# Two feed-forward blocks, fused per hidden block, changed to an up phase and a down phase of Strassen block products

## The reference, cut to what matters

```python
# first block, its end
x = x + merged @ w_out
xn = rms_norm(x, ffn_norm_g)
gate, up = split(xn @ w_gate_up, 2)          # (1024, 1024) @ (1024, 2*2816)
x = x + (silu(gate) * up) @ w_down           # (1024, 2816) @ (2816, 1024)
x = rms_norm(x, final_norm_g)
# second block, its end
x = x + concat([y_sc, y_gdn, y_sb]) @ w_mix_out
h = rmsnorm(x, w_norm_ffn)
u = causal_dwconv(h @ w_ffn_up, w_ffn_conv)  # 3 taps per column
gate, val = split(u, 2)
x = x + (silu(gate) * val) @ w_ffn_down
x = rmsnorm(x, w_norm_final)
```

## Time and profile before

| | us |
|---|---|
| runs shown | 2682.76, 2685.54, 2688.26 |
| median | 2685.54 |
| span of the profiled execution | 2685.9 |
| first feed-forward loop, about 526 to 1206 us of the span | 680 |
| second feed-forward loop, about 1976 to 2660 us | 684 |

### The profile page before, as it was taken

One profiled execution on the slowest core, in us unless ns is written; L12 is line 12 of the kernel. 1 busy time (PEld: TensorE's weight loads), 2 busy tenths in 40 slices (PEclk: granted clock), 3 DMA queues, 4 the chain that ended last, 5 costly groups with the idle time before them and its releaser, 6 DMA issues. The chain is left out here.

```text
span 2685.9 us, 36806 instructions
## 1 busy us (share of the span) xinstructions
PE 2609.6 (97%) x13899; PEld 2081.9 (78%) x13899; DVE 1235.7 (46%) x1717; ACT 680.0 (25%) x1336; POOL 1181.7 (44%) x946
## 2 busy tenths in 40 slices
PE   8999889999999999999999988999999999999998
PEld 6787458888888888887788876845888888888877
DVE  3233543323333333345554155565235555555568
ACT  3200761200000000015233255465131111111123
POOL 4342144244444444463355541515425555555553
PEclk9999999999999999999999999999999999999999
DMA  4111103111111111122111200002101111111112
GB/s 136 44 48 43 48 15 112 32 47 47 50 48 50 47 47 47 51 75 94 32 51 47 59 2 2 18 1 102 51 24 49 49 47 51 47 47 51 47 55 79
DMA packets 92176, 133.83 MB, mean 50 GB/s; under 512 B 9397, under 2 KB 57760, under 8 KB 92072
## 3 DMA queue, kind: packets, MB, share of 16 engines
q1 hardware_dynamic: 89440, 123.86, 15.3%
q10 hardware_dynamic: 2632, 8.51, 0.8%
HBM read 123.92 MB, written 8.42 MB: 49 GB/s over the span
## 5 line engine op out<-in xcount | busy, mean ns | idle before, releaser
L115 POOL TENSOR_TENSOR w_hi<-w_raw,zero 128x512 fp32r<-128x512 f32 x328 | 388.3, 1184 | 989.0 <-PE bank L1100 450.5
L117 POOL TENSOR_TENSOR w_lo<-w_raw,w_hi 128x512 fp32r<-128x512 f32 x328 | 474.9, 1448 | 25.7
L1098 PE MATMUL bank<-xt_hi,w_hi 128*128 128x512 f32 x1232 | 479.5, 389 | 0.8 <-DVE x_sb L1331 0.8
L1100 PE MATMUL bank<-xt_hi,w_lo 128*128 128x512 f32 x1232 | 479.3, 389 | 0.0
L1099 PE MATMUL bank<-xt_lo,w_hi 128*128 128x512 f32 x1232 | 479.3, 389 | 0.0
L1435 DVE TENSOR_TENSOR x_sb<-bank,x_sb 128x512 f32<-128x512 f32 x320 | 221.2, 691 | 203.5 <-PE bank L1134 203.2
L1098 PEld LDWEIGHTS bank<-xt_hi,w_hi 128*128 128x128 f32 x1232 | 231.2, 188 | 49.2 <-DVE x_sb L1331 1.2
L1100 PEld LDWEIGHTS bank<-xt_hi,w_lo 128*128 128x128 f32 x1232 | 231.2, 188 | 48.1
L1099 PEld LDWEIGHTS bank<-xt_lo,w_hi 128*128 128x128 f32 x1232 | 231.2, 188 | 48.0
L1393 DVE COPY hidden_raw<-bank 128x512 f32<-128x512 f32 x44 | 30.4, 692 | 326.0 <-PE bank L1100 326.0
L1402 DVE SCALAR_TENSOR_TENSOR hidden_conv<-hidden_raw_conv,cols,hidden_conv 128x1024 f32<-128x1024 f32 x80 | 156.0, 1979 | 6.6 <-ACT hidden_conv L1235 1.3
(11 more groups left out here) (567 smaller groups left out, 4861.3 us busy)
## 6 DMA issues: line engine op xcount, KB each, us to landing
w_raw<-in_w_gate_up_dram SPq DMA_DIRECT2D x88, 256.0 KB, 3.1
w_raw<-in_w_ffn_up_dram SPq DMA_DIRECT2D x88, 256.0 KB, 3.1
w_raw<-in_w_mix_in_dram SPq DMA_DIRECT2D x64, 256.0 KB, 2.7
w_raw<-in_w_down_dram SPq DMA_DIRECT2D x44, 256.0 KB, 2.6
w_raw<-in_w_ffn_down_dram SPq DMA_DIRECT2D x44, 256.0 KB, 2.6
w_raw<-in_w_in_dram SPq DMA_DIRECT2D x40, 256.0 KB, 2.6
x_sb<-in_x_dram SPq DMA_DIRECT2D x4, 1024.0 KB, 8.4
gate_rows<-gate_sums SPq DMA_DIRECT2D x8, 512.0 KB, 5.5
```

The lines of the kernel that those rows point to most:

```text
L115: pool.tensor_tensor(m.w_hi[:, u, :], m.w_raw[:, u, :], zeros, ALU.add).then_inc(m.hi_done, 1)
L117: pool.tensor_tensor(m.w_lo[:, u, :], m.w_raw[:, u, :], m.w_hi[:, u, :].bitcast(F32), ALU.subtract).then_inc(m.split, 1)
L1098: pe.matmul(m.psum[b][:, :], u_hi[:, col], m.xt_hi[:, k, tok], start=k == 0, stop=False)
L1100: mm = pe.matmul(m.psum[b][:, :], u_lo[:, col], m.xt_hi[:, k, tok], start=False, stop=k == KD - 1)
```

## The change

Both calls of `mlp_stage` change in the same way. The loop over hidden blocks is replaced by two phases, each cut by Strassen's scheme: a product of 2x2 block matrices is made of seven block products (M1 to M7) of sums and differences of blocks instead of eight.

**Up phase.** 22 steps q (gate and up half of each hidden block), each in four units k, so 88 units. A unit takes one w_raw slice (rows k and k+4 of the weights, 256 columns), POOL makes five 128-column block sums of it (`sums`, three instructions, 640 elements), ACT rounds sums (640) and the two plain blocks (256) into `ring_hi`, POOL takes the rest into `ring_lo` (640 and 256). PE does 7 products of three matmuls with the sums of the transposed tokens, which are made once, in the head. ACT copies three products' banks and DVE adds the rest, eight adds for each q (`corners`). The gated rows of each hidden block go to DRAM (`hidden_between`), and the residual goes to DRAM in the head (`x_mid`). All loops are unrolled. With `conv`, middle tap, side taps and silu are as before (4 side taps of 128x1024 for each q).

**Down phase.** 7 products times 11 pairs of hidden blocks, 77 units, in two column groups c (7 pairs, then 4). A unit's operands are a token-side piece A (from `hidden_between`, stationary) and a weight-side piece B, 128x512 each, loaded from DRAM once for all products. POOL makes the sums that a product needs (`OP_A`, `OP_B`: 10 for each pair), ACT rounds both operands, DVE takes the rest of both (POOL of B for four of the products and even pairs: 24 of the 154), PE does 4 tiles of three matmuls. The banks of a finished product are added to one or two quarters of `acc` (`CORNERS`: 12 for each c, times 4 tiles). `acc` is loaded from `x_mid`.

**Head and end.** The head makes the token sums on DVE and POOL and their halves on ACT and DVE; the first q's products 2 and 4 are done on tokens 0 to 511 alone, then the other half is transposed, then products 5, 3, 1, 7, 6. The stage behind starts from other addresses. Semaphores are shared by both calls.

```diff
+PRODUCTS = (2, 4, 5, 3, 1, 7, 6)
...
+DOWN = (3, 5, 1, 4, 7, 2, 6)
...
+OP_A = {1: ("A11", "A22", ALU.add), 2: ("A21", "A22", ALU.add), 3: ("A11",), 4: ("A22",), 5: ("A11", "A12", ALU.add),
+        6: ("A21", "A11", ALU.subtract), 7: ("A12", "A22", ALU.subtract)}
+OP_B = {1: ("B11", "B22", ALU.add), 2: ("B11",), 3: ("B12", "B22", ALU.subtract), 4: ("B21", "B11", ALU.subtract),
+        5: ("B22",), 6: ("B11", "B12", ALU.add), 7: ("B21", "B22", ALU.add)}
+CORNERS = {1: ((0, 0, ALU.add), (1, 1, ALU.add)), 2: ((1, 0, ALU.add), (1, 1, ALU.subtract)),
+           3: ((1, 1, ALU.add), (0, 1, ALU.add)), 4: ((0, 0, ALU.add), (1, 0, ALU.add)),
+           5: ((0, 1, ALU.add), (0, 0, ALU.subtract)), 6: ((1, 1, ALU.add),), 7: ((0, 0, ALU.add),)}
...
+    def slot_free(eng, n):
+
+        if n >= 5:
+            ge(eng, wused, n - 4 if n <= 8 else n - 3)
+        elif n < 2 or n == (2 if lead is None else 4):
+            eng.wait_ge(m.used, base + 8)
+        else:
+            eng.wait_ge(m.used, base + 16)
+
...
+    def low_on_pool(x, p):
+
+        return x in (2, 3, 4, 5) and p % 2 == 0
...
+            def fetch(p, x):
+                place_, when = home[p, x]
+                if p < FIRST_PAIRS:
+                    ge(sp, wused, 5 if when < 0 else UP_UNITS - KQ + when + 1)
+                elif when is not None:
+                    n = at_unit[0, when[0], when[1]]
+                    ge(sp, lod, dve_lows(n))
+                    ge(sp, wlo, pool_lows(n))
+                if x[0] == "A":
+                    ge(sp, hid_out, 32 * (p + 1))
+                sp.dma_start(piece[p, x][:, :], piece_source(p, x)).then_inc(raw_in[p % FIRST_PAIRS].sem, 16)
...
+                fetch(p, "A12")
+            ge(sp, x_out, 16 * NT)
+            ge(sp, hid, 2 * FI)
+            fetch_acc(1, 1, 0)
...
-            split_slices(m, pool, loop, 12 * (FI - 2))
...
+            def sums(n):
+                if n >= UP_UNITS:
+                    gi, x, c, p = unit(n)
+                    to = stage[(n - UP_UNITS) % 3]
+                    if n < UP_UNITS + 3:
+                        ge(pool, wlo, 2 * (UP_UNITS - 1 if n == UP_UNITS else UP_UNITS))
+                    else:
+                        ge(pool, lod, dve_lows(n - 3))
+                        ge(pool, wlo, pool_lows(n - 3))
+                    pieces_in(pool, p, PIECES_OF[x])
+                    for side, op in ((0, OP_A[x]), (1, OP_B[x])):
+                        if len(op) == 3:
+                            pool.tensor_tensor(to[:, side, :], piece[p, op[0]][:, :], piece[p, op[1]][:, :],
+                                               op[2]).then_inc(summed.sem, 1)
+                    return
+                u, s = n % RING, n % 3
+                four = m.w_raw[:, u, :].rearrange("p (b n) -> p b n", b=4)
+                to = w_sum[:, s, :].rearrange("p (b n) -> p b n", b=5)
+                if n >= 3:
+                    ge(pool, wlo, 2 * (n - 2))
+                ge(pool, raw_in[u], 16 * (n // RING + 1))
+                pool.tensor_tensor(to[:, 0:2, :], four[:, 0:2, :], four[:, 3:4, :].to_broadcast([P, 2, P]),
+                                   ALU.add).then_inc(summed.sem, 1)
+                pool.tensor_tensor(to[:, 2:4, :], four[:, 1:3, :], four[:, 0::3, :], ALU.subtract).then_inc(summed.sem, 1)
+                pool.tensor_tensor(to[:, 4, :], four[:, 0, :], four[:, 2, :], ALU.add).then_inc(summed.sem, 1)
+
...
+            sums(0)
+            for n in range(4):
+                sums(n + 1)
+                low(n)
+            for k in range(KQ):
+                ge(pool, x_f, KD + 2 * k + 2)
+                pool.tensor_tensor(d6[:, k, :], xf[:, k, :], xt_hi_f[:, k, T[1]], ALU.add).then_inc(x_sum.sem, 1)
+            for k in range(KQ):
+                pool.tensor_tensor(xf[:, KQ + k, :], xf[:, KQ + k, :], b22[:, k, :], ALU.add).then_inc(x_sum.sem, 1)
+            for k in range(KQ):
+                ge(pool, x_hi, 25 + k)
+                pool.tensor_tensor(d6_lo[:, k, :], d6[:, k, :], d6_hi[:, k, :].bitcast(F32), ALU.subtract).then_inc(x_sum.sem, 1)
+            for n in range(4, N):
+                if n + 1 < N:
+                    sums(n + 1)
+                low(n)
             if nxt is not None:
...
-            with pe.Fori(0, FI - 2) as i:
-                def wait_bank(b):
-                    pe.wait_ge(ev_d if b % 2 else ev_a, 4 * i + b // 2 + 1)
-                    pe.wait_ge(dn_ev, 16 * i + b + 1)
-                up(loop + 12 * i, wait_bank)
...
+            def product(q, k, x):
+                n = KQ * q + k
+                r, bank, col = slot(n), m.psum[bank_of(q, x)], slice(W_COL[x] * P, (W_COL[x] + 1) * P)
+                hi, lo = x_op(x, k)
+                if q == 0:
+                    x_ready(pe, x, k)
+                if k == 0 and q >= (2 if x == 2 else 1):
+                    corner_bank_free(q - (2 if x == 2 else 1), x)
+                pe.matmul(bank[:, :], ring_hi[r][:, col], hi, start=k == 0, stop=False)
+                pe.matmul(bank[:, :], ring_hi[r][:, col], lo, start=False, stop=False)
+                mm = pe.matmul(bank[:, :], ring_lo[r][:, col], hi, start=False, stop=k == KQ - 1)
+                if x == 6:
+                    mm.then_inc(wused.sem, 1)
+                elif k == KQ - 1:
+                    mm.then_inc(mdone.sem, 1)
+
...
+            for q in range(1, 2 * FI):
+                for k in range(KQ):
+                    ge(pe, wlo, 2 * (KQ * q + k + 1))
+                    for x in PRODUCTS:
+                        product(q, k, x)
...
+            def tile_product(n, t, first_, last_, done):
+                gi, x, c, p = unit(n)
+                r, bank, tok = slot(n), m.psum[4 * (gi % 2) + t], slice(t * P, (t + 1) * P)
+                pe.matmul(bank[:, :], ring_hi[r][:, tok], ring_hi[r][:, HALF:], start=first_, stop=False)
+                pe.matmul(bank[:, :], ring_lo[r][:, tok], ring_hi[r][:, HALF:], start=False, stop=False)
+                mm = pe.matmul(bank[:, :], ring_hi[r][:, tok], ring_lo[r][:, HALF:], start=False, stop=last_)
...
+            def high(n):
+                r = slot(n)
+                if n >= UP_UNITS:
+                    gi, x, c, p = unit(n)
+                    slot_free(act, n)
+                    ge(act, summed, sums_made(n))
+                    pieces_in(act, p, PIECES_OF[x])
+                    for side, op in ((0, OP_A[x]), (1, OP_B[x])):
+                        src = stage[(n - UP_UNITS) % 3][:, side, :] if len(op) == 3 else piece[p, op[0]][:, :]
+                        act.activation(ring_hi[r][:, side * HALF:(side + 1) * HALF], src, ACT.Copy).then_inc(whi.sem, 1)
+                    return
+                u, s = n % RING, n % 3
+                slot_free(act, n)
+                ge(act, summed, 3 * (n + 1))
+                act.activation(ring_hi[r][:, 256:896], w_sum[:, s, :], ACT.Copy).then_inc(whi.sem, 1)
+                act.activation(ring_hi[r][:, 0:256].rearrange("p (b n) -> p b n", b=2),
+                               m.w_raw[:, u, :].rearrange("p (b n) -> p b n", b=4)[:, 0::3, :], ACT.Copy).then_inc(whi.sem, 1)
...
+            def put_hidden(i):
+                for c in range(2):
+                    ge(act, hid, 2 * i + c + 1)
+                    act.dma_start(hid_dram[2 * i + c], mix[:, c, :]).then_inc(hid_out.sem, 16)
...
+                act.dma_start(x_mid[t * P:(t + 1) * P, :], x_sb[:, t, :]).then_inc(x_out.sem, 16)
...
+            for n in range(5, N):
+                high(n)
+                if n % 4 == 1 and n < UP_UNITS + 4:
+                    copy_corners((n - 5) // 4)
+                if n >= 7 and n % 4 == 3 and n < UP_UNITS + 4 and conv:
...
+            for k in range(KQ):
+                ge(dve, x_f, KD + 2 * k + 2)
+                dve.tensor_tensor(xt_lo_f[:, k, T[1]], xt_hi_f[:, k, T[1]], b22[:, k, :], ALU.subtract).then_inc(x_dif.sem, 1)
+                ge(dve, x_hi, 9 + k)
+                dve.tensor_tensor(m.xt_lo[:, KQ + k, T[1]], b22[:, k, :], m.xt_hi[:, KQ + k, T[1]].bitcast(F32),
+                                  ALU.subtract).then_inc(x_lo.sem, 1)
+            for k in range(KQ):
+                ge(dve, x_sum, k + 1)
+                dve.tensor_tensor(xf[:, k, :], xf[:, k, :], b22[:, k, :], ALU.add).then_inc(x_dif.sem, 1)
+            for k in range(KQ):
+                ge(dve, x_hi, 13 + k)
+                dve.tensor_tensor(m.xt_lo[:, k, T[1]], xt_lo_f[:, k, T[1]], m.xt_hi[:, k, T[1]].bitcast(F32),
+                                  ALU.subtract).then_inc(x_lo.sem, 1)
+            for k in range(KQ):
+                ge(dve, x_hi, 17 + k)
+                dve.tensor_tensor(xf_r[:, k, :], xf[:, k, :], d1_hi[:, k, :].bitcast(F32), ALU.subtract).then_inc(x_lo.sem, 1)
+            for k in range(KQ):
+                ge(dve, x_hi, 21 + k)
+                dve.tensor_tensor(xf_r[:, KQ + k, :], xf[:, KQ + k, :], d7_hi[:, k, :].bitcast(F32),
+                                  ALU.subtract).then_inc(x_lo.sem, 1)
...
```

(41 more changed lines are left out.)

964 lines of the change are left out of this document (539 added, 425 removed).

## The result

The changed kernel takes 2727.84 us (median of 4 runs, 2722.16 to 2734.19) beside 2684.15 us for the kernel before on the same chip (4 runs, 2682.68 to 2688.26): a ratio of 1.0164, 95% interval 1.0144 to 1.0184. It is slower by 1.6%, where 2664 us (0.8% faster) was forecast. The profiled execution has a span of 2720.4 us, 34.5 more than before.

A forecast was written before the change was run, and what follows sets the result against it. PE's matmuls were taken to bound the kernel; from the 2685.9 us span, -179.6 for matmuls, +44 taps, +66 down phases, +30 heads and +18 turns gave -21.6: 2664 us. Overall range 2590 to 2735, likeliest case 2600 to 2680.

The forecast's parts named there:

- What it removes: Both calls: 396 fewer matmuls each at 0.2267 us, -179.6 us in all.
- Up phase, POOL: First call's up phase: POOL's 34.6 us per hidden block stays hidden under PE's 38.1; cost 0, bounds 0 and 10.
- Up phase with taps: Second call's up phase: side taps slow POOL to 42.1 us per block, 4.0 above PE; +44 us.
- Above: POOL stands still while DVE does what takes 12.7 us alone: Upper bound for the second call's up phase with taps: 8.1 us per block, 90 us.
- Rival 4: PE's clock falls where it starves, half the second up phase at 1.2 GHz: +165, 2829 us; chance 0.04.
- PEclk below 0.95: Sign in the profile's stretches that PE's granted clock had fallen, pointing to Rival 4.
- Head: Each call's head: 38 us from last residual add to last product against PE's 23; +15 a call, +30.
- Down phase: Both down phases: bound by DVE, kept slow by POOL, 243 us each; +33 a call, +66.
- Turn: From up to down phase: late banks and gating ahead of lows; +6 first call, +12 second, +18 together.
- End of the first call: Each call's end keeps its chain, last product done tile by tile: 0, bounds -3 and +3.
- Undisturbed prices: DVE instructions with SBUF source: 0.59 us by the documentation, said to agree with the trace's undisturbed ones.
- rival 2: POOL and DVE take turns, every two-input DVE instruction stopping POOL: 2771 us, range 2691 to 2771; chance 0.20.

The follow-up runs named there:

- e1: Changed kernel with POOL waiting once per up-phase unit for its own last sum, before the first low: 2702.84 us, ratio 1.0062 to the kernel before.
- e6: Changed kernel with e1's wait in every second unit only: 2695.36 us (one run).
- e8: Changed kernel with e1's wait, e7's move, the heads' POOL two-input work on DVE and the second up phase's five-sum lows (units 8 to 87) on DVE: 2623.09 us.
- e11: e8 with the five-sum lows of each call's first four units also moved from POOL to DVE: 2615.02 us, ratio 0.9738 to the kernel before.
- e7: Changed kernel with the down phases' A sums of products 1, 7 and 6 moved from POOL to DVE: 2711.22 us.

## Why the prediction was wrong

A gain of 0.8% was forecast and a loss of 1.6% measured, 56 us apart. Four steps failed: the price of the taps in the second up phase, the head's first weights, and two that the sum had at nothing, PE's clock behind long waits and the end of the first call.

**What it removes: right.** The matmul count is exact, and the phases without POOL or DVE trouble run at 0.2267 us.

**Up phase, POOL: right.** Cost 0 was forecast; 3 us were measured (403 against 400), with POOL busy 360.5 us, 34.3 a block against the 34.6 worked out. Two of the 3 are one held gating product (575.58), whose step took 21.1 us.

**Up phase with taps: this step was wrong in size, and half in mechanism.** Forecast +44, measured +72. "POOL gets through 8 splits (9.3 us alone) in 16.9 us, so it loses 7.5 us per block" is what happens when nothing is held: e1 shows 42.9 us a block against 42.1. But the kernel before could not show what came on top. Its POOL waits between the two halves of each split and rests half of the time. The changed POOL runs for up to 62 us without a gap, and six of the 88 taps stop DVE for 14 to 19 us. I had asked how much the two slow each other and never whether one could be shut out. The statement "Above: POOL stands still while DVE does what takes 12.7 us alone" looked for the worst case on the wrong engine.

**PE's clock: put at nothing.** Rival 4 had a chance of 0.04, and "PEclk below 0.95" was to be its sign. It came: 0.93 in the second up phase, 0.77 and 0.70 in the heads. The clock did not fall at POOL's short waits, as that rival had it (e6, with waits of up to 1.6 us in most steps, has 1.00), but at the six of about 10 us, and it cost some 10 of the 72 us. It goes with the holds: e8 has 1.00 in this phase.

**Head: this step was wrong too.** Forecast 38 us from the last residual add, measured 52.2 and 55.2, so 31 us over in the two calls. The step that failed is "Now 24 matmuls stand ahead of the transposes (5.4 us)". They took until 518.8, 18.0 us after the add, as they wait for POOL, which makes the first four units of weights at 4.4 to 4.9 us each and can't start before the projection has left the ring:

```profile
507.19 0.50 PE L1358 MATMUL bank<-xt_hi,ring_hi 128*128 128x512 f32 x1 [1.94 <-POOL ring_lo L1268]
512.07 0.58 PE L1358 MATMUL bank<-xt_hi,ring_hi 128*128 128x512 f32 x1 [3.22 <-POOL ring_lo L1268]
516.04 0.80 PE L1358 MATMUL bank<-xt_hi,ring_hi 128*128 128x512 f32 x1 [1.25 <-POOL ring_lo L1268]
```

So DVE's chain began 20 us after the add instead of 7. I had priced the x operands of the head and taken its weights as ready. e11 took 4.2 and 2.9 us of it back. The chain behind that (27 us forecast) took 23 on DVE, and POOL's d_lo ended 5 later still (548.95), its first one held for 5.03 us. Only then could POOL make the next unit of weights, ready at 552.95, and the next step began at 553.0. In these gaps PE's granted clock also falls to 0.50, 1.2 GHz (matmuls 0.43 us apart instead of 0.23, from 502 to 505, 512 to 519 and 530 to 543); 36 matmuls at the slow pace are 36 x 0.20 = 7 us in the first head. The last third of them cost nothing, since PE still waited 2 us for POOL at the end; the rest I did not separate.

**Down phase: the size was right, the bound half.** With the turn, +39 and +45 were forecast, +34 and +42 measured. But "The bound is DVE, kept slow by POOL" is the wrong way round for products 1, 7 and 6 in the first column group: e7 gave DVE more to do there and was faster. In the second group it is right, by the trace (DVE without a pause, POOL waiting for it), and e7 gained next to nothing there. That the sizes agree is partly luck: the first call's last product takes 6.0 us a unit where 4.2 were forecast, since its first tile has to wait for all four units, and the other products less. The two readings differ little in price, because it is one shared thing that both wait for. A sum on POOL and a low on DVE take 1.28 and 0.68 us alone and 1.70 together, so the pair is 1.96 / 1.70 = 1.15 times as fast as in turn.

**Turn: about right.** The first two product groups of the second call's down phase take 3.42 and 3.70 us a unit instead of 2.77 and 2.72, 11 us against 12; in the first call there is nothing to see of the 6.

**End of the first call: put at 0, cost 7.** The kernel before goes from its last down products into the next stage with waits of 0.3 us in all. In the changed one PE waits 10.4 us there, in three pieces, for DVE's last adds to `acc`. Here is the longest:

```profile
1208.98 0.79 PE L2064 MATMUL bank<-xt_hi,w_hi 128*128 128x512 f32 x1 [5.04 <-DVE acc L1798]
```

The granted clock is 0.52 and 0.55 behind it. From the last down product to the second head's last residual add it is 734.3 us instead of 727.6. No experiment takes this up. The end of the second call is unchanged (6.9 us instead of 7.3).

**Undisturbed prices.** The prediction calls its 0.59 us borne out by undisturbed instructions of two SBUF inputs. The earlier trace rows has 0.68 for them, 15% more.

Together: 31 us in the heads, 31 in the up phases, -8 in the down phases and turns and 7 at the end of the first call are 61 us, where 56 lie between the forecast span and the measured one. The -5 that are left I can't assign to one step; 1.4 of them lie ahead of the first head and behind the last product. The time lies in my range and on the side of rival 2, at 2728 between its 2691 and 2771. But "every two-input instruction of DVE stops POOL" is not how it got there: in the worst moments it was POOL that stopped DVE.

## What to carry to other kernels

Where one engine's two-input work hides behind another's, count the pair as one resource: the times of both alone, added up and divided by 1.15 (measured for instructions of 512 elements), and give the work to the engine that needs less of it, which here was DVE although DVE was busier. A filler engine that never pauses is a risk of its own: leave it pauses. A wait on its own result in every second or fourth unit was enough (runs of 12 and 22 us), one in every eighth (36 us and more) was not, and one before each instruction cost more than it gave, at about 0.12 us each. And when a change takes a stage's first operands from a stage that was full, price its first units one by one; both heads lost more than the steady state of the first call did.
